# Head norms and rotary embedding of a grouped attention: from the attention block into the end of the projection block before it

## What is computed

```python
def _rms(x, g):
    return x * lax.rsqrt(jnp.mean(x * x, axis=-1, keepdims=True) + EPS) * g

# layer 0 ends: x = layer_norm(ALPHA * x + gate * (mixed @ a_w_out))
# layer 1:
p = x_in @ w_in                        # latent rows: q (2048), k (512), v (512), gate (2048)
kvc = c_in @ w_in[:, o_q:...]          # context rows: k (512), v (512) only
k = _rms(k.reshape(.., 4, 128), k_norm)     # both kinds of row
q = _rms(q.reshape(.., 16, 128), q_norm)
q, k = _rope_2d(q, *pos), _rope_2d(k, *pos) # latent rows only
out = (softmax(q k^T / sqrt(128)) v) * silu(gate)
```

## Time and profile before

| what | value |
|---|---|
| time, median of 3 runs | 4289.64 us (4287.26 to 4293.28) |
| the profiled execution | 4295.89 us, span 4294.1 us |
| PE busy | 3893.7 us, 91% of the span |
| DVE, ACT, POOL busy | 35%, 15%, 13% |
| mean granted clock of TensorE | 0.963 |
| `out_a` hands over to `att_c` | PE idle 7.1 us, first matmul of `att_c` at 1728.65 us |
| rotary work in `att_c` | POOL 1729.06 us to its last store at 1806.49 us |
| `att_c` on PE | until about 1956 us |

### The profile page before, as it was taken

One profiled execution on the slowest core, in us unless ns is written; L12 is line 12 of the kernel. 1 busy time (PEld: TensorE's weight loads), 2 busy tenths in 40 slices (PEclk: granted clock), 3 DMA queues, 4 the chain that ended last, 5 costly groups with the idle time before them and its releaser, 6 DMA issues. The chain is left out here.

```text
span 4294.1 us, 59484 instructions
## 1 busy us (share of the span) xinstructions
PE 3893.7 (91%) x25244; PEld 1976.4 (46%) x25244; DVE 1502.5 (35%) x2698; ACT 647.5 (15%) x1330; POOL 553.9 (13%) x802
## 2 busy tenths in 40 slices
PE   8799997898949999887999999898988989989998
PEld 1245443344524444353444444453436667665443
DVE  0079996383211210432200013344533333332321
ACT  0000000102230110032110000143431122111000
POOL 0011110111100000110000012342103222231100
PEclk9899998999979999998999999998999999999999
DMA  8778875873265555625555578637763343333562
GB/s 294 258 263 324 294 276 195 288 264 107 86 254 199 169 183 169 217 73 206 179 167 168 166 251 304 204 121 237 257 224 93 92 122 98 92 102 139 201 224 104
DMA packets 357979, 822.59 MB, mean 192 GB/s; under 512 B 25468, under 2 KB 61652, under 8 KB 350796
## 3 DMA queue, kind: packets, MB, share of 16 engines
q1 hardware_dynamic: 257040, 485.08, 34.3%
q0 software_dynamic: 72544, 275.55, 17.8%
q10 hardware_dynamic: 28136, 58.22, 3.5%
HBM read 698.00 MB, written 120.77 MB: 191 GB/s over the span
## 5 line engine op out<-in xcount | busy, mean ns | idle before, releaser
L1029 PE MATMUL gemm_a_g_ps<-store_w,turned 128*128 128x512 f32 (+1 forms) x1152 | 455.5, 558 | 1.9 <-PEq L203 1.9
L812 DVE SCALAR_TENSOR_TENSOR pmods_acc<-pmods_w,cond,pmods_acc 128x512 f32<-128x512 f32 x570 | 402.8, 748 | 22.8 <-issue 0.9
L1029 PE MATMUL out_c_g_ps<-store_w,turned 128*128 128x512 f32 (+1 forms) x1024 | 399.3, 552 | 0.0
L1029 PEld LDWEIGHTS gemm_a_g_ps<-store_w,turned 128*128 128x128 f32 x1152 | 209.4, 191 | 247.5 <-issue 247.5
L2246 PE MATMUL scan_g_ps<-store_w,turned 64*64 64x512 f32 x2048 | 297.1, 623 | 19.1 <-PEq L1382 14.0
L1029 PEld LDWEIGHTS out_c_g_ps<-store_w,turned 128*128 128x128 f32 x1024 | 184.5, 190 | 213.8 <-issue 213.8
L1029 PE MATMUL att_a_g_ps<-store_w,turned 128*128 128x512 f32 x512 | 240.4, 603 | 12.8 <-PEq L3035 8.9
L1029 PE MATMUL gemm_hq_g_ps<-store_w,turned 128*128 128x512 f32 x512 | 222.3, 597 | 7.2 <-PEq L3035 7.2
L1029 PE MATMUL out_a_g_ps<-store_w,turned 128*128 128x512 f32 x512 | 221.8, 595 | 1.1 <-PEq L203 1.1
L1029 PE MATMUL out_a_g_ps<-store_w,turned_c 128*128 128x512 f32 x512 | 220.2, 592 | 0.0
L1029 PE MATMUL feat_g_ps<-store_w,turned 128*128 128x512 f32 x384 | 182.1, 623 | 21.5 <-ACT feat_stage L1629 13.6
(11 more groups left out here) (434 smaller groups left out, 4960.3 us busy)
## 6 DMA issues: line engine op xcount, KB each, us to landing
store_w<-in_w_in SPq DMA_DIRECT2D x160, 1024.0 KB, 5.5
pmods_w<-in_w_mod POOLq DMA_DIRECT2D x38, 2048.0 KB, 10.5
mods_w<-in_w_mod SPq DMA_DIRECT2D x48, 1024.0 KB, 9.3
store_w<-in_a_w_in SPq DMA_DIRECT2D x48, 1024.0 KB, 7.9
store_w<-in_c_w_in SPq DMA_DIRECT2D x48, 1024.0 KB, 5.1
store_w<-in_a_w_out SPq DMA_DIRECT2D x32, 1024.0 KB, 5.1
s_feat<-feat_o POOLq DMA_DIRECT2D x16, 1536.0 KB, 8.9
store_w<-in_w_branch SPq DMA_DIRECT2D x48, 512.0 KB, 3.6
```

Source lines behind the costliest of these rows:

```text
L812: v.scalar_tensor_tensor(a, src, x, a, ALU.mult, ALU.add)
L1029: mm = pe.matmul(out, act_tile(q * kq + k, tb), self.store.slot[i % self.store.NS][:, k, :width], start=(q == 0 and k == 0), stop=(q == 3 ...
```

## The change

`out_norm_project` takes a function `rope`. For `out_a` it is `rope_c`, whose DVE and POOL programs are put behind everything that those engines do in the block. Its buffers are `z0`, `z1` (items), `z2` (temporary) and `z3` (tables). Since an item must fit into 128x2048, the latent rows are now two items each, 16 query heads and then 4 key heads: six items for four. Before a load, POOL waits until 12 copies of `proj_c` have landed (items 0 to 3) or 14 (items 4 and 5). `att_c` gets no first programs, and its `lead` is 10 for 86.

```diff
-def rotate_heads(nc, name, items, cos_sin, gains=None):
+def rotate_heads(nc, name, items, cos_sin, gains=None, buffers=None, wait_source=None):
...
-        buf = [st.enter_context(nc.sbuf_tensor(f"{name}_x{s}", [P, big], F32)) for s in range(2)]
...
+        if buffers:
+            buf, tmp = buffers[0:2], buffers[2]
+            cs = buffers[3][:, 0:4 * d].rearrange("p (j t d) -> p j t d", j=2, t=2)
+            gb = buffers[3][:, 4 * d:6 * d].rearrange("p (j d) -> p j d", j=2)
...
         def load(pool, n):
             arr, H = items[n][:2]
+            if wait_source:
+                wait_source(pool, n)
...
+        def wait_copies(eng, count):
+            for s in range(4):
+                eng.wait_ge(stored[s], 16 * ((count + 3 - s) // 4))
+        rope_programs = rope(st, z, wait_copies) if rope else None
         block = st.enter_context(nc.Block())
...
+            if rope:
+                rope_programs[0](v)
...
             for what, tb in centres:
                 pool.wait_ge(x_stored[tb], 16)
+            if rope:
+                for tb in turns:
+                    after(pool, "dve", "turn", tb)
+                    after(pool, "act", "turn", tb)
+                rope_programs[1](pool)
...
+        def rope_c(st, z, wait_copies):
+            gains = ((C_Q, 16, 0), (C_K, 4, 1))
+            items = [(rows(proj_c, tb)[:, a:a + 128 * h].rearrange("t (h c) -> t h c", h=h), h, 128, tb, [(0, h, gi)])
+                     for tb in LAT for a, h, gi in gains]
+            items += [(rows(proj_c, tb)[:, C_K:C_V].rearrange("t (h c) -> t h c", h=4), 4, 128, None, [(0, 4, 1)]) for tb in (2, 3)]
+            return rotate_heads(nc, "rope_c", items, (C["rope128"][0], C["rope128"][1]), [I["c_q_norm"][0], I["c_k_norm"][0]], z,
+                                lambda eng, n: wait_copies(eng, 12 if n < 4 else 14))(st)
...
-                         col(1, 1), col(1, 0), without_func(c_first))
+                         col(1, 1), col(1, 0), without_func(c_first), rope=rope_c)
...
-        attend_and_project(nc, "att_c", store, ident, GroupedPlan(proj_c, mix_c, tiled), 128 ** -0.5, 128, xc, c_gate, 86, rope)
+        attend_and_project(nc, "att_c", store, ident, GroupedPlan(proj_c, mix_c, tiled), 128 ** -0.5, 128, xc, c_gate, 10)
```

More of the change, by code:

```diff
@@ L430, in make @@
     def make(st):
-        buf = [st.enter_context(nc.sbuf_tensor(f"{name}_x{s}", [P, big], F32)) for s in range(2)]
-        tmp = st.enter_context(nc.sbuf_tensor(f"{name}_t", [P, big], F32))
-        cs = st.enter_context(nc.sbuf_tensor(f"{name}_cs", [P, 2, 2, d], F32))
-        gb = st.enter_context(nc.sbuf_tensor(f"{name}_g", [P, 2, d], F32))
+        if buffers:
+            buf, tmp = buffers[0:2], buffers[2]
+            cs = buffers[3][:, 0:4 * d].rearrange("p (j t d) -> p j t d", j=2, t=2)
+            gb = buffers[3][:, 4 * d:6 * d].rearrange("p (j d) -> p j d", j=2)
+        else:
+            buf = [st.enter_context(nc.sbuf_tensor(f"{name}_x{s}", [P, big], F32)) for s in range(2)]
+            tmp = st.enter_context(nc.sbuf_tensor(f"{name}_t", [P, big], F32))
+            cs = st.enter_context(nc.sbuf_tensor(f"{name}_cs", [P, 2, 2, d], F32))
+            gb = st.enter_context(nc.sbuf_tensor(f"{name}_g", [P, 2, d], F32))
         stat = st.enter_context(nc.sbuf_tensor(f"{name}_stat", [P, 4, hmax], F32))
@@ L1093, in out_norm_project @@
 def out_norm_project(nc, name, store, ident, mixed, turned_in, w_out, x_src, x_dst, gate_rows, gate_bias, gain, bias,
-                     scale, shift, projections, rms=False):
+                     scale, shift, projections, rms=False, rope=None):
     with ExitStack() as st:
```

## The result

The changed kernel takes 4301.6 us in the median of 11 runs (4290.42 to 4321.59), the kernel before 4289.72 in 11 runs beside them (4282.68 to 4302.63). The ratio is 1.0031, 95% interval 1.002 to 1.0042, so the change makes the kernel slower by 13.3 us, between 8.6 and 18 (the two medians alone lie 11.9 us apart). Forecast were 13.3 us and 4303.0.

A forecast was written before the change was run, and what follows sets the result against it. PE, busy 91% of the span, was taken to bound the kernel. 33.7 lost - 30.2 gained + 9.8 lost = 13.3 us slower: 4295.89 to 4309.2, the median 6.25 lower, 4303.0; range 4292 to 4311.

The forecast's parts named there:

- The tail: End of `out_a`: the rotary chain ends late, PE starts `att_c` at 1762.4 against 1728.65, 33.7 us lost.
- Q0: Rotary chain in `out_a`: query item of row tile 0, 16 heads, 20.4 us on DVE from 1682.2 to 1702.6.
- POOL's store waits: Rotary chain: POOL makes an item's power only after the preceding store lands; query stores 5.5 and 5.0 us, keys 3.5, 2.65.
- The tables: Start of the rotary chain: from POOL's first load to DVE's first operation 8.5 us, between 5.3 and 10.45.
- The load of Q1: Rotary chain: load of the query item of row tile 1, from 1708.3, about 6 us.
- K0's store: Rotary chain: store of the key item of row tile 0, 3.5 us from issue to release, releasing POOL at 1718.1.
- What `att_c` gives back: PE in `att_c`: load wait 10.1, low clock 2.0 and 21 score waits 18.1 us go, 30.2 us gained.
- the price of the copies: Lead of 10 in `att_c`: seven Silu copies ahead of `prob_t` delay values, three by 1.89, four by 1.03: 9.8 us lost.
- The drain: Rival, chance 0.03: table switches stop ACT 1.38 us beyond their record at all seven copies in `att_c`: +23, 4313.
- the chain set by DVE: Rival, chance 0.07: in the rotary chain stores land while DVE works, 21.2 us lost, sum +0.8, 4290.4.
- the free copies: Rival, chance 0.14: ACT's table loads hide in `att_c`, no price at the copies; 3.5 us slower, 4293.
- the longer tail: Rival, chance 0.12: stores and tables in `out_a` run at slow rows, 39 and more, clock low longer: +19 to +23, 4311.

The follow-up runs named there:

- tables first: The changed kernel with the cosine, sine and gain table loads issued ahead of POOL's wait for the twelve copies, not behind two item loads: ratio 0.9995 to the kernel before.
- the run with the old lead: The changed kernel with the lead of 86 put back for 10, rotary work still in `out_a`: ratio 1.0061 to the kernel before.
- eight buffers: The changed kernel with eight stage buffers in the attention blocks for four: ratio 1.0011 to the kernel before.
- covered: The changed kernel with queries projected first, values last, and rotary items in the order their rows are ready: 4264.36 us, ratio 0.9928 to the kernel before.
- no rotary work: The changed kernel with head norms and rotation of q and k left out of the computation: ratio 0.9946 to the kernel before.
- power first: The changed kernel, but POOL makes the next item's power before waiting for the current item's store to land: ratio 1.001 to the kernel before.
- leads of 56 and 86: The one of 56: the changed kernel with a lead of 56 for 10, ratio 1.0001 to the kernel before. For 86 see the run with the old lead.
- before with lead 10: The kernel before with lead 10 for 86, rotary work still at the start of `att_c`: ratio 1.0112 to the kernel before.
- covered with lead 56: The covered kernel with a lead of 56 instead of 10: ratio 0.9933 to the kernel before.

## Why the prediction was right, point by point

**The tail, 33.7 us forecast, 37.2 measured.** The mechanism held: start at copy 12 (1673.7 forecast, 1673.88), Q0 in 20.4 us (1683.85 to 1704.28), POOL's store waits ahead of the powers. Four terms were too small. The tables came 10.0 us after the first load, where I had taken 8.5 between bounds of 5.3 and 10.45, nearly the 10.45 of before though only half the bytes of items lay ahead. The DMA engines moved 286 GB/s in these 10 us and 290 in those of before, so nearly as many bytes: weight loads had taken the place of the missing ones. That this is the reason was not tested apart. The load of Q1 took 6.9 us, not 6. K0's store took 6.15 us to its release, not 3.5, and so held up Q1's power for about 1 us. The load of Q1 isn't the reason, as it had landed when DVE began at 1716.34, 0.7 us after the issue of that store; weights and ACT's last copies moved after it, but which of them it was isn't shown, and with the tables first the same store took 3.35 us. And from the issue of the last store to PE's start went 5.5 us, not 3.7. The two query stores were quicker instead, 4.95 and 4.53 for 5.5 and 5.0. One reading was wrong without harm to the sum: the projection still had 48 us to run when the chain began, not "27 us", which is about the length of one job (27.5 us between the copies' issues at 1668.07 and 1695.54).

**What `att_c` gives back, 30.2 us forecast.** The 25.3 us measured and the price of the copies below make 30.3. Its parts were seen singly: the load wait gone, the 21 score waits gone, which with the value waits in exchange make the 14.0 us of the lead. The prediction's own terms for it are 18.1 - 9.8 = 8.3; the 13.1 expected before the run with the old lead already used the measured price of the copies.

**The price of the copies, 9.8 us forecast, 5.0 measured.** This term was mis-sized by half. I had priced all seven by `att_a`'s 1.89 us, whose tiles among the exponentials all stand behind a wait for a stage buffer. The first four of `att_c` have none, and their table load ran ahead of the tile. With 1.28 us less, the two with one unit behind the prob cost 0.55 each (the record shows 0.39) and the two with two units nothing; the other three cost 1.04, 1.89 and 1.03. The eight buffers showed it. The drain that the Trainium skill adds to a table load ("ScalarE: Activation LUTs", section "What ACT_TABLE_LOAD costs") is not in these rows either: the load at 1918.56 follows its tile, and the copy starts 1.29 us after it.

**The sum.** Tail +3.5, copies -4.8, the rest about -0.8: the stretch came out at 11.1 where 13.3 stood. The nearness of 13.3 to the timed 13.3 is partly luck, since the errors have both signs. Of the rivals, the chain set by DVE and the free copies are refuted by the rows above (before, by the way, three table loads for copies stood in the spread, at 1836.88, 1850.27 and 1943.86, not two); of the longer tail (39 and more) the measured one came within 2 us. Its argument that the clock is low longer after 40 us of rest does not hold (last section).

**Not explained.** The profiled execution's span is 25.7 us above that of before, of which the stretch and what lies ahead of it hold 12. The rest arose in the blocks of features and scan, whose code is unchanged. Little of it is in the medians: the profiled execution of the changed kernel is the slowest of its eleven, 20.0 us above their median, that of before only 6.25 above its own, and these two differ by just about the 14 us. The scan's gate matmuls span 726.9 us in the kernel before and 738.4 in the changed one:

```profile
L2266 PE MATMUL scan_g_ps<-store_w,turned x2048: 586/590/1113, 3215.4 to 3953.8; 64*64 64x512 f32 x187
```

With the lead of 86, where the rotary work is moved just the same, it was 725.8 us, without any rotary work 735.1, and in the covered order 738.9. So it doesn't follow the move. In the changed kernel PE stands 18.3 us in six stops ahead of the matmuls of L2447, the longest 6.4, for which the profile names no releaser; before they were 9.3 us in five (L2427 there), with the lead of 86 3.8 in four. That is most of the 11.5 us, and the cause of these stops isn't known.

## What to carry to other kernels

Work that is moved from under cover costs what sticks out at its new place: ask when its inputs are ready and how much of the bounding engine's work is left then, here 48 us for a chain of 90. The gain lies in the order of the producers: with the inputs of the longest item first, the same move is 31 us faster than before in place of 13 slower. A store that an engine waits for before it serves the next item is as much of such a chain as its arithmetic.

## What the runs showed that was not expected

A copy with its table load of 1.28 us, one filler unit behind the prob, costs PE 1.89 us if a second wait (here for a stage buffer) stands ahead of the copy, and 0.55 if only the wait for the tile does. Without the second wait the table load ran ahead of the tile. No other kind of second wait was tried.

The barrier at the block's end took PE 1.1 us beyond the last landing before, when the last transfer was ACT's. With POOL's store last (issued at 1761.07, 2.4 us to landing) it took 3.1; three kernels show 5.5 us each from that store's issue to PE's start. Where ACT's transfer was the last again (no rotary work, covered) it took 1.2. Why isn't settled.

PE's clock after a stop: in the changed kernel, after 44 us of rest, the granted clock was 0.50 for 6.0 us, the lower of TensorE's two levels (1.2 GHz for 2.4), and the ten units of lead took 11.6 us, where full clock would make it 8.6. Before, after 7.1 us of rest at the same place, the matmul records of `att_c` stood 0.86 us apart until 1733.83 and 0.43 from there on (granted clock 0.52 in the earlier trace rows): 5.2 us, and 11.2 for the same ten units. It would be wrong to read from this pair that a longer rest costs more. Other executions after 40 to 44 us of rest had the low clock for 2.9 us (eight buffers), 3.3 (power first, tables first) and 5.8 to 6.0 (leads of 56 and 86), and those after 7.4 us (no rotary work, covered, before with lead 10, covered with lead 56) for 5.2 to 6.1. So the low clock lasted 3 to 6 us, and its length did not follow the rest.

That explains how far two readings of `att_c` can differ. Executions of the same `att_c` code (changed, no rotary work, power first, tables first, covered) gave 199.9 to 201.2 us; without the ten units of lead, which took 10.3 to 11.6 us, each of the five is 189.6.
